# Softmax scores of the second query tile as three products of high and low parts, with the retention's gating product on GpSimd

## The reference

```
proj = h @ w_in[l]
q_r, k_r, v_r, g_r, q_m, k_m, v_m = jnp.split(proj, offsets, axis=-1)
...
o_r = head_group_norm(o_r, ret_norm_gain[l], ret_norm_bias[l]) * jax.nn.silu(g_r)
y_ret = o_r @ w_ret_o[l]
qm = rms_norm(heads(q_m, MOBA_HEADS), moba_q_gain[l])
km = rms_norm(heads(k_m, MOBA_HEADS), moba_k_gain[l])
...
s_own = jnp.einsum('bhqd,bhkd->bhqk', q_i, k_own).astype(jnp.float32) * scale
p = jax.nn.softmax(...)
```

## Time and profile before

| | |
|---|---|
| median of 3 runs | 451.29 us (451.16 to 451.46) |
| time of the profiled execution | 451.38 us |
| its span in the trace | 449.6 us |
| granted clock, mean | 1.00 |
| PE, PEld busy | 99%, 83% of the span |
| DVE, ACT, POOL busy | 77%, 64%, 24% of the span |
| data moved | 100.23 MB, mean 223 GB/s |

### The profile page before, as it was taken

The page is one execution under the profiler, slowest core; times in us unless marked ns, Lnnn a source line. Parts: engine busy times, 40 slices in busy tenths (PEclk is TensorE's granted clock), DMA queues, the critical chain, the costliest instruction groups (busy, mean ns, idle before and its releaser), DMA issues.

```text
span 449.6 us, 5565 instructions
## 1 busy us (share of the span) xinstructions
PE 445.0 (99%) x2101; PEld 373.5 (83%) x2101; DVE 344.4 (77%) x402; ACT 287.4 (64%) x377; POOL 106.7 (24%) x71
## 2 busy tenths in 40 slices
PE   8999999999999999999999999999999999999997
PEld 6899988888888888888887888888888888888886
DVE  4789994886689849777585478589999999987423
ACT  6885453055996857245346268499999999996300
POOL 0100021499360021210210004333333333300000
PEclk9999999999999999999999999999999999999999
DMA  8997658547999625998586343977878878773102
GB/s 288 422 390 258 257 191 233 141 177 214 247 266 276 270 95 179 292 300 305 188 239 265 104 187 118 338 223 233 239 233 242 239 243 246 249 253 126 56 0 93
DMA packets 64071, 100.23 MB, mean 223 GB/s; under 512 B 50224, under 2 KB 51120, under 8 KB 54704
## 3 DMA queue, kind: packets, MB, share of 16 engines
q1 hardware_dynamic: 63632, 98.36, 68.4%
q0 software_dynamic: 416, 1.57, 1.2%
HBM read 86.81 MB, written 1.05 MB: 195 GB/s over the span
## 4 chain that ended last, share of the span: by engine, by line
PE 86%; DMA 5%; DVE 4%; ACT 2%; issue 1%; SPq 1%
PE bank L544 11%; PE bank L543 11%; PE bank L542 11%; PE bank L789 8%; PE bank L791 8%; PE bank L790 8%; PE bank L833 4%; PE bank L836 4%; PE bank L834 4%; DMA w_raw<-weights_dram 4%; PE bank L729 2%; PE bank L727 2%; PE bank L728 2%; DVE w_pair L1119 2%; DMA area<-area 1%
## 5 line engine op out<-in xcount | busy, mean ns | idle before, releaser
L1119 DVE TENSOR_TENSOR w_pair<-w_raw,w_pair 128x2048 fp32r<-128x2048 f32 x73 | 177.5, 2449 | 32.2 <-ACT w_pair L853 31.9
L853 ACT ACTIVATE w_pair<-w_raw 128x2048 fp32r<-128x2048 f32 x73 | 139.4, 1923 | 43.6 <-PE bank L544 19.7
L542 PE MATMUL bank<-w_pair,h_hi 128*128 128x512 f32 x192 | 75.1, 391 | 0.0
L544 PE MATMUL bank<-w_pair,h_lo 128*128 128x512 f32 x192 | 74.8, 389 | 0.0
L543 PE MATMUL bank<-w_pair,h_hi 128*128 128x512 f32 x192 | 74.7, 389 | 0.0
L789 PE MATMUL bank<-w_pair,h_hi 128*128 128x512 f32 x160 | 62.3, 389 | 0.0
L791 PE MATMUL bank<-w_pair,h_lo 128*128 128x512 f32 x160 | 62.3, 389 | 0.0
L790 PE MATMUL bank<-w_pair,h_hi 128*128 128x512 f32 x160 | 62.3, 389 | 0.0
L1468 DVE SCALAR_TENSOR_TENSOR area<-area,col 128x256 f32<-128x256 f32 x88 | 44.8, 560 | 3.9 <-ACT area L1068 2.9
L542 PEld LDWEIGHTS bank<-w_pair,h_hi 128*128 128x128 f32 x192 | 36.1, 188 | 7.4
L543 PEld LDWEIGHTS bank<-w_pair,h_hi 128*128 128x128 f32 x192 | 36.1, 188 | 7.4
(11 more groups left out here) (171 smaller groups left out, 761.4 us busy)
## 6 DMA issues: line engine op xcount, KB each, us to landing
w_raw<-weights_dram SPq DMA_DIRECT2D x73, 1024.0 KB, 5.7
w_raw<-weights_dram SPq DMA_DIRECT2D x8, 256.0 KB, 5.3
w_raw<-weights_dram SPq DMA_DIRECT2D x4, 512.0 KB, 9.1
ys<-x_dram SPq DMA_DIRECT2D x2, 512.0 KB, 9.0
xs<-x_dram POOLq DMA_DIRECT2D x1, 1024.0 KB, 6.3
area<-decay_dram SPq DMA_DIRECT2D x1, 768.0 KB, 8.6
out_dram<-ys SPq DMA_DIRECT2D x3, 256.0 KB, 2.0
xs<-x_chan_dram SPq DMA_DIRECT2D x1, 512.0 KB, 6.8
```

The source lines that it names most:

```text
L542: mm(o, s_hi, hi[:, kk, :], start=(first and kk == 0), stop=False)
L544: ins = mm(o, s_lo, hi[:, kk, :], start=False, stop=(last and kk == 3))
L853: A(w_parts(n, r)[0], raw[r][:, :], ACT.Copy).then_inc(hi_ready, 1)
L1119: tt(lo, raw[r][:, :], hi.bitcast(f32), ALU.subtract).then_inc(lo_ready, 1)
```

## The change

PE makes the 128x256 product of each head in three fp32r products of high and low parts. `score_high(g)` on ACT makes the high parts of the queries (128x512, second tile only) and keys (128x1024) of a group, `score_low(g)` on DVE the low ones; PE waits for `score_split` before head 0 of a group. The four gating products go from DVE's list to POOL's, behind `split_words(3)`. ACT's `copy_block` waits for them, since it overwrites the gates. `ret_high` goes behind `score_high(0)`, and `ret_low` from block V_M0 to block V_M1.

```diff
+        k_parts = [part[:, KT:2 * KT, :] for part in (a_hi, a_lo)]
+        q_parts = [part[:, 2 * KT:2 * KT + 4, :].rearrange("p k (i s) -> p (k i) s", i=2) for part in (a_hi, a_lo)]
...
+            pool.wait_ge(gates_joined, 4)
+            for j in range(4):
+                pool.wait_ge(ret_affine, j + 1)
+                k = slice(2 * j, 2 * j + 2)
+                nc.gpsimd.tensor_tensor(ret_t[:, k, :], ret_t[:, k, :], g_t[:, k, :], ALU.mult).then_inc(ret_gated, 1)
+
...
-                    mm(o[:, P:P + SEQ], qm_t[:, h, P:SEQ], km_t[:, h, :], start=False, stop=True)\
-                        .then_inc(unit_made, 1)
+                    if j == 0:
+                        pe.wait_ge(score_split, 2 * g + 2)
+                    split_product(o[:, P:P + SEQ], [part[:, h, :] for part in q_parts], [part[:, h, :] for part in k_parts],
+                                  False, True).then_inc(unit_made, 1)
...
             def copy_block(b, dst):
+                act.wait_ge(ret_gated, 2 * (b - V_M0) + 2)
...
+            def score_high(g):
+                heads = slice(4 * g, 4 * g + 4)
+                act.wait_ge(sums_qk, 8)
+                act.wait_ge(heads_joined, 2 * JOIN_ORDER.index(g) + 2)
+                A(q_parts[0][:, heads, :], qm_t[:, heads, P:SEQ], ACT.Copy).then_inc(score_hi_ready, 1)
+                act.wait_ge(keys_scaled, 2 * g + 2)
+                A(k_parts[0][:, heads, :], km_t[:, heads, :], ACT.Copy).then_inc(score_hi_ready, 1)
...
-                V_M0: lambda: (ret_high(0), ret_high(1)), V_M1: lambda: (scale_keys(1), exps(0)),
+                V_M1: lambda: (scale_keys(1), score_high(1), exps(0)),
...
                     scale_keys(0)
+                    score_high(0)
+                    ret_high(0)
+                    ret_high(1)
...
+            def score_low(g):
+                heads = slice(4 * g, 4 * g + 4)
+                dve.wait_ge(score_hi_ready, 2 * g + 1)
+                tt(q_parts[1][:, heads, :], qm_t[:, heads, P:SEQ], q_parts[0][:, heads, :].bitcast(f32), ALU.subtract)\
+                    .then_inc(score_split, 1)
+                dve.wait_ge(score_hi_ready, 2 * g + 2)
+                tt(k_parts[1][:, heads, :], km_t[:, heads, :], k_parts[0][:, heads, :].bitcast(f32), ALU.subtract)\
+                    .then_inc(score_split, 1)
...
-            def ret_gate(g):
-                dve.wait_ge(gates_joined, 4)
-                for j in range(2 * g, 2 * g + 2):
-                    dve.wait_ge(ret_affine, j + 1)
-                    k = slice(2 * j, 2 * j + 2)
-                    tt(ret_t[:, k, :], ret_t[:, k, :], g_t[:, k, :], ALU.mult).then_inc(ret_gated, 1)
...
-                K_M1: lambda: join_heads(0), V_M0: lambda: (ret_gate(0), ret_gate(1)),
+                K_M1: lambda: join_heads(0), 
...
-                V_M1: lambda: normalise_probs(0), GATE_R0: lambda: normalise_probs(1),
+                V_M1: lambda: (score_low(1), ret_low(0), ret_low(1), normalise_probs(0)), GATE_R0: lambda: normalise_probs(1),
...
                 if b == V_M0:
+                    score_low(0)
                     join_heads(3)
-                    ret_low(0)
-                    ret_low(1)
                     join_heads(1)
```

More of the change, by code:

```diff
@@ L252, in hybrid_layer @@
         keys_scaled = sem("keys_scaled")
+        score_hi_ready = sem("score_hi_ready")
+        score_split = sem("score_split")
         gate_planes_ready = sem("gate_planes_ready")
```

## The result

The changed kernel took 454.42 us (median of 8 runs, 453.78 to 457.75), the kernel before 451.19 us beside it (8 runs). The ratio is 1.0076, 95% interval 1.0062 to 1.009: slower by 0.8%, 3.2 us. The prediction was 453.7 us, the range 451.8 to 456.0.

What follows compares the result with a forecast made beforehand. PE, busy 99% of the span, was taken to bound the kernel. The terms -0.56, +1.0, +0.9, +0.1 and +0.8 gave +2.3 us with rounding on the profiled 451.38: 453.7 us, range 451.8 to 456.0.

Steps and rivals of the forecast that it cites:

- -0.56: PE's score products: three fp32r products cost 0.36 us against 0.43 in float32, 0.07 less for each of 8 heads.
- +1.0: First scores (group 0): low parts ready at 145.5, PE wants them at 144.56 and waits about 1.0 us.
- +0.9: Half 28: lo(28) ends at 172.7, PE wants it at 171.8 and waits 0.9 us.
- +0.1: Half 29: lo(29) ends at 178.2, when PE wants it; PE hardly waits, 0.1 us in the sum.
- +0.8: Attention's output: joins of the first probabilities follow lo(29) by 11.7 us, to 189.9; PE waits 0.8 us more.
- The reading of turns: DVE instructions on two SBUF inputs and POOL instructions don't run together; the first runs to its end, then the other.
- The rival in which the port is not in the way: Gates run mostly beside DVE's instructions; lo(25) ends at 140.0, shift +0.7 us, time 452.1; chance 0.20.
- Only PE's gain: Rival: DVE's idle time before lo(28) takes in the new instructions, lo(29) no later; 450.8 us; chance 0.07.
- The price of a gate: Each POOL gating product of 128x512 taken as 1.04 us, from a copy of 128x1024 words; range 0.5 to 1.9.
- dearer gates: Rival: gates on POOL cost 1.2 to 1.9 us each, giving 454.3 to 457.1 us (454.7 at 1.3); chance 0.24.
- the start of the stretch: POOL is free for the first gate at 133.82, when the second L444 copy ends in the profile before.
- The reserves: Time before PE notices lateness: lo(28) 1.4 us, lo(29) 1.3 us, joins of the first probabilities 0.4 us.

Runs made afterwards that it cites:

- the idle products: Kernel before plus four 128x512 products on POOL behind split_words(3), on constants into unused memory, nobody waiting: 453.54 us beside 451.52.
- the reordered kernel: Changed kernel with gating products on DVE and, in blocks V_M1 and GATE_R0, splits put behind score and softmax work: 450.67 us beside 451.6 for the kernel before.
- the earlier transposes: Changed kernel with SP issuing the transposes of the first probabilities behind the load of half 32, not 33: 453.51 us beside 451.52 for the kernel before.
- the last reordered one: Changed kernel, gates on POOL, with splits behind softmax work in blocks V_M1 and GATE_R0: 453.87 us beside 451.9 for the kernel before; run again, 453.69 beside 451.63.
- the run with float32 scores: Changed kernel with float32 scores, no score_high or score_low, gates still on POOL, ret_high and ret_low late: 451.23 us beside 451.52 for the kernel before.

## Why the prediction came out

**The sign and the mechanism.** The forecast was +2.3 us on the profiled execution, made of -0.56, +1.0, +0.9, +0.1 and +0.8. In the profile after, by the shift of PE's starts, the terms are -0.5 for the heads, +1.6 before the first scores, +1.2 at half 28 (its second product starts 2.44 later than before; the last product ahead of it, at 172.36, was 1.22 later), nothing visible at half 29, and some +1.0 at the joins. Another 0.1 was there before the stretch, and 0.2 came after it. That makes the 3.6 of the span. The three gaps stand at the three places named. The prediction's heads, -0.56, lie between the -0.5 here and the -0.63 that PE gains where nothing holds it up.

**The port.** The reading of turns held. It rested on three lengths, and the idle products showed it alone. The rival in which the port is not in the way is out: lo(25) ended at 144.47 against its 140.0. *Only PE's gain* is out for this order of the code, and is what the reordered kernel gave (450.67 against 450.8).

**The price of a gate.** I took 1.04 us; alone it is 1.29. The Trainium skill, page "GPSIMD Engine Reference", section 3.1 "Elementwise — side-by-side cycle accounting", by which I had estimated 1.3 for a two-input operation, agrees with 1.29. But the term did not grow by 4 x 0.25 = 1.0, as my sensitivity of 0.4 us for each 0.1 would have it. The stretch from the start of the first gate to the end of the low parts was 133.82 to 145.5 in the prediction, 11.68 us. In the profile after it is 134.25 to 146.21, 11.96; in three other executions with these gates (the changed kernel again, the earlier transposes, the last reordered one) 11.94 or 11.95. So the whole stretch was 0.28 too short. In a turn with a join, 1.74 us from start to start, 0.64 is the join's and 1.10 the gate's. Only the first gate, which started on an idle port, shows the full 1.29. That the rest of it overlaps DVE's instruction fits these lengths, but was not measured apart. The rival *dearer gates*, with the page's 1.3, gave 454.7, nearly the measured 454.42, for a reason that held only in part. That is luck.

**The step that was mis-sized: the start.** The prediction took the start of the stretch from the one execution before, 133.82. It is not fixed. In the 13 profiles the second pair of L444 (L448) copies, which the gates stand behind, starts anywhere from 129.29 to 132.93, though the code ahead of it is the same. Most of that moves PE too and costs nothing; what counts is the distance to PE's first score product. Before it was 144.33 - 129.74 = 14.59 us, and it is 14.59 or 14.60 in seven of the profiles. In four it is 14.20 to 14.45, and 14.20 (144.41 - 130.21) in the profile after: the pair started 0.47 later and PE 0.08. Two kernels with both halves of the change have the usual distance, that with the earlier transposes and the last reordered one, and their gap before the scores is 1.1 us; in the changed kernel's two profiles, with 14.20 and 14.24, it is 1.5 and 1.4.

The chain to those copies can be followed. ACT's joining of the retention's words (L904, L917) waits for the retention's transposes and starts at 118.45 instead of 117.99; its next split, DVE's lo(22), DVE's products for the last key block and POOL's copies follow one another, each 0.4 to 0.5 later. The kernel before has 0.4 to 1.4 us of reserve behind that chain and mostly swallows this. In the changed kernel PE waits for the chain, and it goes straight into the time.

In the remaining two profiles the distance is 12.96 (gates on DVE, 455.33 us) and 12.56 (the reordered kernel with gates on POOL, 455.50 us). In the second of them:

```profile
127.32 2.29 DVE L1143 TENSOR_TENSOR w_pair<-w_raw,w_pair 128x2048 fp32r<-128x2048 f32 x1 [1.13 <-ACT w_pair L865]
131.14 1.29 DVE L1272 TENSOR_TENSOR xs<-bank,inv_qk 128x512 f32<-128x512 f32 x2 [1.53 <-POOL inv_qk L436]
```

```profile
127.46 3.65 POOL L436 TENSOR_TENSOR inv_qk<-inv_qk,neg_half 128x8 f32<-128x8 f32 x1
```

POOL's small power (the inverse root for the last key block) came 0.14 us behind lo(22), ended 1.5 after it, and DVE's products for the last key block waited 1.53 for the power. In the profile after it began at 127.19, 0.03 ahead of lo(22), and took 1.64. I read this as the same taking of turns: a turn lost by a tenth of a microsecond put some 2 us into the chain. POOL was late there because its first pair of copies was: it waits for the transposes of the first queries, which SP issued late. In just three profiles, these two and the one after, SP's issue of the load ahead of them took 1.4 to 1.5 us; in the other ten it took 0.58. That the port held the power is read from these starts and ends, not tried by itself.

**The sum, mended.** lo(28) came 0.9 later than predicted (173.63 against 172.7): 0.43 for the start, of which PE shares 0.08, 0.28 for the turns, 0.2 for DVE's list from there on. The joins followed lo(29) as forecast (190.93 against 189.9). With 0.3 for restarts and small shifts behind, 2.3 + 0.9 + 0.1 + 0.3 = 3.6.

**The reserves.** They were read rightly at 1.4 us for lo(28), and in the run with float32 scores that reserve is still whole. What the prediction did not say is that the two halves of the change share the room of 2.5 us between lo(25) and the first scores: apart +0 and +1, together +3.2. The alternative that pays was in reach by the same rows. DVE waited 5.50 us for ACT ahead of lo(28) while lo(27), which PE did not need yet, stood in front of `neg_max`.

**Still open.** Why the transposes land at different times, and why SP's issue of one load took 1.5 us in three of 13 profiles, no run shows. Both profiled executions of the changed kernel lie above their medians (455.08 against 454.42, 455.27 against 454.56). A start nearer the usual one in the other executions would fit that, but none of them was profiled.

## What to carry to other kernels

Before work goes from DVE to GpSimd, look for two-input instructions of DVE in the same stretch: there the two take turns, and DVE gets its time back only while it stands idle. Price two halves of a change against the room that they share together, not each against the whole. Read a time in another execution against the engine that waits, not against the start of the trace. And where an engine idles for another that waits for it in turn, first try to put the short work that feeds the other ahead of the long work that nobody is waiting for; here that turned a loss of 0.2% into a gain of 0.15%.

## What the runs showed of the hardware

- A product of two different 128x512 float32 tiles on GpSimd: 1.29 us alone, some 1.10 within turns. One of a broadcast 128x256 tile with itself: 0.85 within turns.
- DVE and POOL take turns when both have work waiting: 1.52 us for each of four DVE products of 0.68, 1.48 for the POOL products beside them. DVE's copies of 16-bit words take part too (1.84 each instead of 0.75), and a 128x8 instruction of DVE beside a POOL copy took 1.37 instead of 0.17.
- POOL's small power (128x8, for the last key block) takes 1.64 us in eleven of the profiles, and 3.65 and 3.79 in the two where DVE's lo(22) had begun by then (0.14 us ahead, and at the same recorded time); it then ended 1.5 us after lo(22). The other way round it hardly holds DVE: begun 0.03 us ahead of lo(22) in the profile after, it left it at 2.32 us instead of 2.29.
- The one with 3.65, of the reordered kernel with gates on POOL (455.5 us), is the only one of the 13 profiles with a mean clock below 0.999: 0.996. PE waited 2.9 us before the scores and ran at full speed for some 1.5 us behind the wait; the windows by 5 us (busy time of PE, PEld, DVE, ACT and POOL with counts, granted clock, DMA share, GB/s) and two of its product starts are:

```profile
145.00:150.00 5.00, 2.25 (x16) 2.25 (x17) 4.97 (x6) 4.18 (x8) 1.01 (x1) 0.93 1.01 424
150.00:155.00 5.00, 5.00 (x20) 4.11 (x19) 4.83 (x21) 4.47 (x10) 0.00 (x0) 0.73 0.12 51
```

```profile
150.91 0.63 PE L553 MATMUL bank<-w_pair,h_hi 128*128 128x512 f32 x1
151.34 0.63 PE L554 MATMUL bank<-w_pair,h_lo 128*128 128x512 f32 x1
```

Products came 0.43 us apart instead of 0.23, which is the 1.2 GHz level, for some 3.2 us: 1.5 us more on top of the wait. After the 1.46 us gap of the changed kernel the granted clock stayed at 1.00. It was not a single event: another execution of that kernel on the same chip (454.94 us) had a mean clock of 0.996, its longest on another chip (457.07 us) 0.993, and the longest of the changed kernel (457.75 us) 0.996. Where the clock fell in these was not recorded. That the gap brought the clock down is the order of events, not shown by a run of its own.
